# A hybrid encoder layer with sixteen experts: the first expert's weights are loaded behind the last output tile

## What is computed

```python
def trunk(x, ...):
    h = rms_norm(x, norm_mix_g[layer])
    x = x + mixer(h, ...)            # ends in: concatenate([att, hgo]) @ w_out
    h = rms_norm(x, norm_ffn_g[layer])
    x = x + expert_choice_ffn(h, w_router[layer], w_gate[layer], w_up[layer], w_down[layer])
    return rms_norm(x, final_norm_g)

def expert_choice_ffn(h, w_router, w_gate, w_up, w_down):
    n_tok = B * T
    cap = max(1, EC_CAPACITY * n_tok // N_EXPERTS)
    aff = jax.nn.softmax((flat @ w_router).astype(jnp.float32), axis=-1)
    g, idx = lax.top_k(aff.T, cap)
    xs = flat[idx]
    hid = jax.nn.silu(jnp.einsum('ecd,edf->ecf', xs, w_gate)) * jnp.einsum('ecd,edf->ecf', xs, w_up)
    out = jnp.einsum('ecf,efd->ecd', hid, w_down) * g[..., None].astype(h.dtype)
    y = jnp.zeros((n_tok, D), h.dtype).at[idx.reshape(-1)].add(out.reshape(-1, D))
```

## Time and profile before

| what | us |
|---|---|
| median of three runs | 2191.64 |
| the profiled execution's own time | 2191.68 |
| its span, from the first to the last instruction | 2189.9 |
| the last tile's `y_rows` store is issued | 1216.58 |
| the last instruction of VectorE in the mixer starts | 1254.45 |
| the first load of an expert's weights is issued | 1257.08 |
| TensorE's first matmul with an expert's weights | 1274.52 |
| the last transfer of results is issued | 2179.62 |

### The profile page before, as it was taken

One profiled execution on the slowest core, in us unless ns is written; L12 is line 12 of the kernel. 1 busy time (PEld: TensorE's weight loads), 2 busy tenths in 40 slices (PEclk: granted clock), 3 DMA queues, 4 the chain that ended last, 5 costly groups with the idle time before them and its releaser, 6 DMA issues. The chain is left out here.

```text
span 2189.9 us, 43441 instructions
## 1 busy us (share of the span) xinstructions
PE 2008.1 (92%) x16048; PEld 1753.0 (80%) x16048; DVE 1468.9 (67%) x2769; ACT 1111.4 (51%) x1983; POOL 290.1 (13%) x419
## 2 busy tenths in 40 slices
PE   7999998899897899798899379999999999999996
PEld 6877876777786777676788279999999999999995
DVE  5466575666666577676348857777777777778876
ACT  5322322456565523265322156767666667667774
POOL 1101101000000011100122001111111111111234
PEclk9999998999998999999999689999999999999998
DMA  5211100100002122211233088787778787778995
GB/s 180 83 31 31 35 26 16 38 20 24 19 6 82 48 59 83 64 53 53 106 114 114 36 273 260 249 258 249 259 247 262 245 260 248 255 255 301 348 323 188
DMA packets 183465, 317.82 MB, mean 145 GB/s; under 512 B 11872, under 2 KB 82016, under 8 KB 183328
## 3 DMA queue, kind: packets, MB, share of 16 engines
q1 hardware_dynamic: 169984, 281.06, 38.1%
q0 software_dynamic: 8608, 30.68, 5.6%
q10 hardware_dynamic: 4736, 4.19, 0.6%
HBM read 279.97 MB, written 35.91 MB: 144 GB/s over the span
## 5 line engine op out<-in xcount | busy, mean ns | idle before, releaser
L2267 DVE TENSOR_TENSOR we_lo<-raw,we_hi 128x1024 fp32r<-128x1024 f32 x384 | 466.1, 1224 | 188.8 <-ACT we_hi L2192 187.8
L2158 PE MATMUL psum<-x_parts,we_hi 128*128 128x384 f32 x2048 | 585.0, 360 | 3.1 <-DVE we_lo L2267 3.1
L2160 PE MATMUL psum<-x_parts,we_lo 128*128 128x192 f32 x2048 | 513.4, 251 | 0.0
L2192 ACT CAST we_hi<-raw 128x1024 fp32r<-128x1024 f32 x384 | 400.1, 1054 | 156.6 <-PE psum L2160 93.3
L2160 PEld LDWEIGHTS psum<-x_parts,we_lo 128*128 128x128 f32 x2048 | 392.0, 191 | 0.6
L2158 PEld LDWEIGHTS psum<-x_parts,we_hi 128*128 128x128 f32 x2048 | 385.5, 188 | 4.1 <-issue 3.5
L599 PE MATMUL psum<-hT_hi,w_hi 128*128 128x512 f32 x512 | 215.5, 421 | 0.8 <-issue 0.8
L601 PE MATMUL psum<-hT_hi,w_lo 128*128 128x512 f32 x512 | 203.6, 398 | 0.0
L600 PE MATMUL psum<-hT_lo,w_hi 128*128 128x512 f32 x512 | 202.9, 396 | 0.0
L599 PE MATMUL psum<-hP_hi,w_hi 128*128 128x512 f32 x256 | 109.5, 428 | 15.9 <-DVE w_lo L572 11.6
L601 PEld LDWEIGHTS psum<-hT_hi,w_lo 128*128 128x128 f32 x512 | 97.8, 191 | 22.0
(11 more groups left out here) (313 smaller groups left out, 3774.0 us busy)
## 6 DMA issues: line engine op xcount, KB each, us to landing
raw<-in_w_gate SPq DMA_DIRECT2D x128, 512.0 KB, 4.7
raw<-in_w_up SPq DMA_DIRECT2D x128, 512.0 KB, 6.7
raw<-in_w_down SPq DMA_DIRECT2D x128, 512.0 KB, 5.0
w_raw<-in_w_in SPq DMA_DIRECT2D x96, 256.0 KB, 2.9
y_rows<-x SPq DMA_DIRECT2D x12, 512.0 KB, 2.6
h_rows<-h SPq DMA_DIRECT2D x12, 512.0 KB, 2.9
y<-y_rows SPq DMA_DIRECT2D x12, 512.0 KB, 7.9
w_raw_s<-in_w_in SPq DMA_DIRECT2D x16, 256.0 KB, 2.9
```

Of the source, the lines that this page charges most:

```text
L2158: pe.matmul(out[:, 0:2 * SLOTS], w_hi[:, s, at], x_parts[p][:, k, :, :], start=(k == 0), stop=False, skip_group_check=True)
L2160: mm = pe.matmul(out[:, SLOTS:2 * SLOTS], w_lo[:, s, at], x_hi[p][:, k, :], start=False, stop=(k == DT - 1), skip_group_check=True)
L2192: act.copy(w_hi[:, n % PARTS, :], raw[:, s, :]).then_inc(hi.sem, 1)
L2267: dve.tensor_tensor(w_lo[:, n % PARTS, :], raw[:, n % RAW, :], w_hi[:, n % PARTS, :].bitcast(F32), ALU.subtract).then_inc(lo.sem, 1)
```

## The change

The experts' `raw`, `we_hi` and `we_lo` become a fourth layout of the 64 KB piece that holds the output weights at the mixer's end. A new class `FirstWeights` holds the eight semaphores of `raw` (a set of their own, which is cleared when the whole program ends, behind one more barrier) and the addresses of the loads. SyncE issues the first eight loads in the mixer: behind the `y_rows` store of the last tile, when TensorE has counted its last `sum` in `m_used`, and ahead of that tile's `h_rows` store. In the experts the first three splits stand ahead of the first expert's `turn` on ScalarE and VectorE. SyncE's loads of the first pair are written out ahead of the loop and begin with the ninth unit.

```diff
 build():
+        weights = {"raw": ([P, RAW, FF], F32), "we_hi": ([P, PARTS, FF], F32R), "we_lo": ([P, PARTS, FF], F32R)}
+        of_s, of_p, of_o, of_e = overlay(nc, whole, 64 * 1024, (
+            {"hT_hi": ([P, DT, T_SAMPLE], F32R), "hT_lo": ([P, DT, T_SAMPLE], F32R)},
...
+            {"wo": ([P, 2, 2, HALF, D], F32R)}, weights))
+        first = FirstWeights(whole.enter_context(semaphores(nc, "r")), w_gate, w_up, of_e["raw"])
...
+class FirstWeights:
+    def __init__(self, sem, w_gate, w_up, raw):
+        self.raw_in = [Signal(sem(f"raw_in{s}"), 2 * 16 * 3 * DT // RAW) for s in range(RAW)]
+        self.w, self.raw = (w_gate, w_up), raw
+    def source(self, e, n):
+        w, h = self.w[n // HALF % 2], n // DT
+        at = (n % HALF) * 2 * P
+        return w[0, e, at:at + 2 * P, h * BLK:(h + 1) * BLK].rearrange("e (a p) f -> p (e a) f", p=P)
+    def place(self, n):
+        return self.raw[:, n % RAW, :].rearrange("p (a f) -> p a f", f=BLK)
+    def loads(self, sp):
+        start_signals(sp, self.raw_in)
+        for n in range(RAW):
+            sp.dma_start(self.place(n), self.source(slice(0, 1), n)).then_inc(self.raw_in[n].sem, 16)
 project_out(), late_loads:
                 sp.wait_ge(added, 2 * t)
                 sp.dma_start(y_dram[at:at + P, :], x1[(t - 1) % 2][:]).then_inc(y_out[(t - 1) % 2], 16)
+                if t == NT:
+                    sp.wait_ge(m_used, 2 * NT)
+                    first.loads(sp)
                 sp.wait_ge(normed, t)
                 sp.dma_start(h2_dram[at:at + P, :], h2[(t - 1) % 2][:]).then_inc(h_out[(t - 1) % 2], 16)
 experts():
-        raw = sb("raw", [P, RAW, FF])
-        w_hi, w_lo = sb("we_hi", [P, PARTS, FF], F32R), sb("we_lo", [P, PARTS, FF], F32R)
+        raw, w_hi, w_lo = of_e["raw"], of_e["we_hi"], of_e["we_lo"]
...
-        raw_in = [Signal(sem(f"raw_in{s}"), 2 * 16 * UNITS // RAW) for s in range(RAW)]
+        raw_in = first.raw_in
...
             body("gather", 0, 0)
+            for n in range(PARTS - 1):
+                body("split", 0, 0, n)
             body("turn", 0, 0)
             body("gather", 0, 1)
-            for n in range(PARTS - 1):
-                body("split", 0, 0, n)
             with eng.Fori(0, LOOPED) as i:
 experts(), sync:
-                start_signals(sp, raw_in)
...
-                        for n in range(UNITS):
+                        for n in range(RAW if begun and p == 0 else 0, UNITS):
                             sp.wait_ge(lo.sem, lo.at(i, p * UNITS + n - RAW))
...
-                with sp.Fori(0, LOOPED) as i:
+                loads(0, False, True)
+                with sp.Fori(1, LOOPED) as i:
                     loads(i, False)
```

More of the change, by code:

```diff
@@ L38 @@
 TOP = 8
+RAW, PARTS = 8, 4
 GROUPS = [0, 96, 64]
@@ L301, in overlay, with mixer_memory @@
     return made
-def mixer_memory(nc, ctx):
+def mixer_memory(nc, ctx, held):
     sb = lambda name, shape, dt=F32: ctx.enter_context(nc.sbuf_tensor(name, shape, dt))
@@ L325, in mixer_memory @@
     o.w_hi, o.w_lo, o.small = w_hi, w_lo, small_o
[L327 to L330, removed]
+    of_s, of_p, of_o = held
     s.hT_hi, s.hT_lo = of_s["hT_hi"], of_s["hT_lo"]
@@ L669, in turning, with mix @@
     return out
-def mix(nc, ctx, x_s, x_p, g_mix, w_in, lq1, lk1, lq2, lk2, subln, lb_cols, hg_norm, w_out, g_ffn, w_router,
+def mix(nc, ctx, held, first, x_s, x_p, g_mix, w_in, lq1, lk1, lq2, lk2, subln, lb_cols, hg_norm, w_out, g_ffn, w_router,
         masks_in, dist_in, ident_in, ident, minus_half, psum, banks, aff, aff_last, shares, index, index_cols, gate_cols, h2_dram, y_dram, turned_dram):
@@ L680, in mix @@
                         "subln": subln, "hg_norm": hg_norm})
-    mem_s, mem_p, mem_o = mixer_memory(nc, ctx)
+    mem_s, mem_p, mem_o = mixer_memory(nc, ctx, held)
     mem_s.pairs = [psum[:, 0:2 * BLK], psum[:, 2 * BLK:4 * BLK]]
@@ L689, in mix @@
     a_p = attention(sem, 1, T_PROMPT, w_in, dist_in, consts, banks, mem_p, h_p)
-    o = project_out(sem, (x_s, x_p), w_out, g_ffn, w_router, consts, banks, mem_o, aff, aff_last, shares, index, index_cols, gate_cols, h2_dram, y_dram, u_p.signals["lo_done"], h_p, a_p)
+    o = project_out(sem, (x_s, x_p), w_out, g_ffn, w_router, consts, banks, mem_o, aff, aff_last, shares, index, index_cols, gate_cols, h2_dram, y_dram, u_p.signals["lo_done"], h_p, a_p, first)
     o_early, o_beside, o_tiles = o.stages
@@ L1594, in attention, with project_out @@
                   "weighed": weighed, "w_turned": w_turned})
-def project_out(sem, xs, w_out, g_ffn, w_router, consts, banks, mem, aff, aff_last, shares, index, index_cols, gate_cols, h2_dram, y_dram, rows, before_h, before):
+def project_out(sem, xs, w_out, g_ffn, w_router, consts, banks, mem, aff, aff_last, shares, index, index_cols, gate_cols, h2_dram, y_dram, rows, before_h, before, first):
     NT = N_TOK // P
@@ L1930, in project_out, with experts @@
     return Heads(None, (early, beside, tiles), (early_loads, late_loads), tensor, scalar, vector, gpsimd, {})
-def experts(nc, ctx, w_gate, w_up, w_down, g_final, ident, minus_half, psum, banks, index_cols, gate_cols, h2_dram, y_dram, out_p, out_s):
-    RAW, PARTS, PAIRS, UNITS = 8, 4, EXPERTS // 2, 3 * DT
+def experts(nc, ctx, first, of_e, w_gate, w_up, w_down, g_final, ident, minus_half, psum, banks, index_cols, gate_cols, h2_dram, y_dram, out_p, out_s):
+    PAIRS, UNITS = EXPERTS // 2, 3 * DT
     Q = DT // 2
@@ L2088, in store, with loads @@
                     sp.dma_start(to, y[:, s, :]).then_inc(y_out[s], 16)
-                def loads(i, late):
+                def loads(i, late, begun=False):
                     for p in range(2):
-                        e = 2 * i + p if late else sp.snap(2 * i + p)
-                        for n in range(UNITS):
+                        e = 2 * i + p if late or begun else sp.snap(2 * i + p)
+                        for n in range(RAW if begun and p == 0 else 0, UNITS):
                             sp.wait_ge(lo.sem, lo.at(i, p * UNITS + n - RAW))
@@ L2097, in loads @@
                             if n < 4 * Q:
[L2098 to L2101, removed]
+                                src, to = first.source(bass.ds(e, 1), n), first.place(n)
                             else:
```

5 lines of the change are left out of this document (3 added, 2 removed).

## The result

The kernel after took 2200.05 us in the median, the kernel before 2192.50 us on the same chip: a ratio of 1.0034, 95% interval 1.0025 to 1.0043. The forecast was 2187.3 us in a range up to 2191.4: wrong in sign, and 12.75 us off. The profiled execution of after took 2198.89 us.

A forecast was written before the change was run, and what follows sets the result against it. TensorE, busy 92% of the span, was taken as the bound, with the hand-over to the experts as the hole. Gather 2.1, splits 1.6 and clock 1.5 less 0.8 at the end made 4.4 us won: 2187.3 us, range 2183.8 to 2191.4.

The forecast's parts named there:

- the first one: Start of the prediction: TensorE never rests behind the hand-over, so moving the first expert's first matmul moves the end equally.
- Loads early: Eight weight loads queued at 1217 in the mixer cost 0; SyncE still waits some 20 us at the mixer's end.
- The gather: Hand-over: the second gather of token rows lands at 1265.6 instead of 1267.66, 2.1 us won, bounds nothing to 4.0.
- The second rival: Hand-over: loads of units 8 to 10 and the blocked issue keep the landing at 1267.7; 2189.4 us, chance 0.14.
- The estimate of 5.4 us to landing: Second gather's time to landing with 1.5 MB beside it where 4.2 MB ran; 5.4 us instead of 8.24.
- The charge of 0.8 us for the blocked issue: GpSimd's issue of the second gather is delayed once by VectorE's splits running beside it, 0.8 us lost.
- locked out for the whole run: Slower rival: VectorE's splits keep GpSimd from issuing gathers until all end; 4.2 us slower, 2195.9 us, chance 0.06.
- The splits: Three weight splits ahead of the turn: the first expert matmul no longer waits for them, 1.6 us won, bounds 1.5 to 1.7.
- The clock: Shorter pause between turn and first expert matmul keeps TensorE at full clock, 1.5 us won, bounds 0 and 1.65.
- The end: Program's end: clearing the loads' own semaphore set behind one more barrier, 0.8 us lost, 0.7 at least.

The follow-up runs named there:

- hold: after_384 with SyncE's loads of the first expert's units 8 to 10 held until both gathers landed; 2187.20 us against 2191.80 of before, ratio 0.9978.
- splits_behind: after_384 with the first expert's first three splits put back behind the first rows' turn, eight loads still early; 2189.57 us, ratio 0.9987 to before.
- hold_one_set: hold with the eight load semaphores taken from the experts' own set, so the second clearing and barrier fall away; 2186.79 us, ratio 0.9975 to before.
- after_384: The kernel after with 384 empty bytes ahead of the 64 KB piece and 640 behind it in the mixer; 2189.57 us against 2191.43 of before, ratio 0.9989.
- warm: hold_one_set with 28 unused transposes of ident on TensorE ahead of its first turn; 2185.22 us, ratio 0.9969 to before.
- weights_128: The kernel before with 128 empty bytes ahead of w_hi and w_lo and 128 behind them; 2199.91 us, ratio 1.0041 to before.
- all_128: The kernel before with 128 empty bytes in each partition ahead of all the mixer's tensors; 2196.03 us in one run.
- experts_128: The kernel before with 128 empty bytes in the experts' memory between the weights and all the rest; 2201.83 us against 2191.76, ratio 1.0054.

## Why the prediction was wrong

**The step that failed** is the first one: "whatever moves the first expert's first matmul therefore moves the end by as much" looked only at the hand-over. The sum takes all that lies ahead of the barrier at its old time, and the diff's moved `overlay` call has no term in it; it was put at nothing without a reason. It was in the diff that the 64 KB piece left its place, and 2,880 matmuls of the mixer read it against `w_hi` or `w_lo`. It cost some 7.5 us; in the two traces all the rest together won 0.3.

**Loads early: free, as said.** VectorE's picking takes as long as before within 0.2 us (the difference grows from 7.35 to 7.57 over it), and SyncE's wait for TensorE behind the mixer shrank from 31.6 us to 22.1, near the 20 forecast. SyncE's waits in after, from 1185 to 1270:

```profile
SPq L823 <- PEq L823: 22.1, 1, 22.1
...
SPq L1746 <- DMA h_rows<-h: 9.8, 1, 9.8
```

**The gather: 2.1 us forecast, 0.4 won** (15.75 us to 15.32 from the picking to the first transpose). The second rival came: the loads of units 8 to 10 take the old ones' place. The estimate of 5.4 us to landing was meant for a gather with 1.5 MB beside it. That it fits a gather left alone is luck: to the first transpose it is 5.6 in `hold` and 5.4 in `splits_behind`. What I missed is that 1.5 MB are enough to be in its way when they start at the same time. From the start of the issue the sum had 0.8 + 5.4 = 6.2 us; in after the landing is 7.82 us after it, by the chain (start us, us, what):

```profile
1266.97 7.82 DMA rows_s<-h_rows,index_s
```

The charge of 0.8 us for the blocked issue was right for the issue itself (1.74 against 0.96); how much of it reaches the rows is seen above in `hold`, 0.28 us. GpSimd was not locked out for the whole run: the issue ended at 1268.71, the splits at 1269.02.

**The splits: 1.6 forecast, 1.62 won** (6.82 to 5.20 from first transpose to first matmul). Not seen: by freeing `raw` early they start the very loads that hold the gather up.

**The clock: 1.5 us won forecast, some 1.4 lost.** After ran its first 6.1 us of expert matmuls at 1.2 GHz (the fourth stretch above), before 3.3 us, at half the speed a loss of 1.4; from the first to the last expert matmul it took 896.36 us, before 894.99. That stretch alone would not show it: in the eight traces that have the hand-over and the experts of before it varies from 894.1 to 897.6. The reason given, that a pause of 1.5 us keeps the clock, does not hold: the turn already runs at half clock, and when the clock comes back varies. With the same 1.5 us behind the turn the half clock ended 6.1 us after the first expert matmul in after, 3.2 after it in `hold_one_set`, and 0.8 and 1.7 before it in `after_384` and `hold`. In all ten traces with the pause of 3.1 us it ended 3.8 to 4.7 us after it, so the short pause gained in some traces and lost in the measured one. The stretch from the first matmul on in `hold`, then in `hold_one_set`, columns as in `warm`:

```profile
1272.50:1278.00 5.50, 5.49 (x39) 1.00 0.64 206
```

```profile
1271.30:1274.60 3.30, 3.23 (x12) 0.50 0.70 205
```

The term lies between some 1.65 us won (no half clock at all) and 1.4 lost, with the same pause, and what decides it is open; I should have taken zero with these bounds, where the prediction had nothing below 0.

**The end: 0.8 us lost forecast, 0.4 measured** (20.73 us from the start of the last expert matmul to the end against 20.36).

**Behind the hand-over TensorE does wait once**, at the last pair's turn, which the long stretch of the earlier trace rows hides as 0.84 us. In `after_384` it is 2.30 us, and 1.4 of the 2.8 us by which it was ahead went there; its two gathers were issued at 1.9 us each instead of 1.1. But kernels with the hand-over of before show as wide a spread: no wait in `weights_128`, and 2.21 us in `all_128`, with issues of 1.0 us. What sets this wait is open. Before, then `after_384`, then `all_128`:

```profile
2046.55 0.33 PE L2135 MATMUL psum<-ident,rows_p 128*128 128x128 f32 x1 [0.84 <-DMA rows_s<-h_rows,index_s]
```

```profile
2045.16 0.33 PE L2160 MATMUL psum<-ident,rows_p 128*128 128x128 f32 x1 [2.30 <-DMA rows_s<-h_rows,index_s]
```

```profile
2050.92 0.33 PE L2136 MATMUL psum<-ident,rows_p 128*128 128x128 f32 x1 [2.21 <-DMA rows_s<-h_rows,index_s]
```

So, even with the mixer left in place, the end follows the first expert matmul only to within some 2 us in a single trace.

## What to carry to other kernels

Read a diff for what it allocates, not only for what it issues: an allocation that moves a tensor shifts all that stand behind it, and the sum needs a term for the matmuls that read them. Put the operands of a matmul of this kind (4-byte, 512 columns) a multiple of 256 bytes apart in a partition, and when a kernel falls behind from its first microseconds on, compare the start-to-start distance of one kind of matmul before looking at any wait. Work that is moved ahead also frees its buffers ahead: ask which transfer that starts, and beside what.

## What the runs showed of the hardware

- Matmuls of 512 columns (4-byte operands) come every 228 to 230 ns (the two kinds of the table; 227 in the experts) where moving and stationary operand lie a multiple of 256 bytes apart, every 232 to 233 at 128 bytes by 256, and in one trace some 230 to 231 at 64. At 128 bytes that is about 2% of these matmuls' time. Matmuls of 384 columns lost 1.7 ns of 197, of 192 columns 0.5 of 88 (`experts_128`). In sum some 7.5 us in the mixer, 11.9 in the experts.
- An indirect gather of rows, issued with 1.5 MB of loads starting beside it, took 7.9 to 8.0 us to its reader, hardly less than the 8.3 beside 4.2 MB before; alone behind another gather it took 5.4 to 5.6.
- GpSimd took 1.71 to 1.74 us to issue that gather beside VectorE's splits, 0.96 without them.
- The granted clock rose 5.0 us into 5.69 us of transposes in `warm`; whether it is full at the first expert matmul varied between kernels with the same instructions around it.
